# Heads before chunks: reordering ScalarE and VectorE at the end of the first block's attention, with one TensorE wait moved later

## The chip, the cores and the metric

The kernel runs on one core of a Trainium2 chip. Its time is the device time of one execution in microseconds (us); the figure compared is the median over runs. TensorE (PE) multiplies, VectorE (DVE) and ScalarE (ACT) prepare its operands and empty its banks, SyncE (SP) issues the loads of weights. Each of these engines works through its own list of instructions in order, and semaphores tie the lists together.

## The reference, cut to what matters

Two transformer blocks follow one another on a sequence of 256 tokens of width 2048. The change lies in the first block, between its input projection and its output projection:

```
h = rmsnorm(x, pre_mix_g)
q_a, k_a, v_a, q_b, k_b, v_b, f_b = split(h @ w_in)
o_a = swa_sink_attention(q_a, k_a, v_a, sinks)        # 16 heads, window of 128
o_b = forgetting_attention(q_b, k_b, v_b, log_f)      # 16 heads, causal, with a decay
mix = concat(rmsnorm(o_a), rmsnorm(o_b)) @ w_out
x = x + rmsnorm(mix, post_mix_g)
```

After it come a gated feed-forward of width 5632 with a causal convolution, and the second block. All of it is float32; the output is the final x.

## The kernel before

**Matmuls in three parts.** A float32 matmul is done as three matmuls of a rounded part and a rest. Every piece of weights (1024 columns on 128 partitions, 512 KB) is loaded into `raw`, rounded into `w_hi` by ACT (line 537) and its rest put into `w_lo` by DVE (line 1067). This is `split(u)` for piece number u; a slot of four is used again once the piece four before it was multiplied. TensorE waits for `lo_ready` of a piece, and multiplies it in 12 or 24 matmuls (lines 1862 to 1864).

**Groups of pieces.** The projections are groups of eight pieces. Group 8, the last of them, holds the second half of the values `v_b`; its products lie in banks 0 and 1 until ACT (`first_values`, line 559) and DVE (`token_out`, line 1093) scale them into `vb`. That emptying is counted by `banks_free`. After group 8 comes the first half of the output projection, `w_out_a`: eight pieces, called W0 to W7 here, of which W0 to W3 go to banks 2 and 3, W4 to W7 to banks 0 and 1. `early` is the number of W0.

**Heads.** The 32 attention heads are a pipeline that is laid between the pieces. On TensorE `head(i)` does the scores of head i (lines 2023, 2026), the turning of the probabilities of head i-2 (line 2037) and the values of head i-3 (lines 2051 to 2053). On DVE it does `bias(i)` (lines 1184 to 1194), then the reciprocal of i-1 (line 1207) and the scaling of output i-3 into `work` (line 1212). On ACT it copies the turned probabilities of i-2 out of their bank (line 645) and takes the exponentials of i (lines 657 to 660). So the values of head i-3 on TensorE wait (`out_done`) until DVE has scaled the output of head i-4, which on DVE stands behind `bias(i-1)`.

**Chunks.** The outputs of heads 0 to 15, once scaled by their norm, are turned by TensorE (`out_phase`, line 2103) into banks 2 and 3, and taken out as the chunks 0 to 7 of the output projection's left operand: `sT_hi` by ACT (line 723), `sT_lo` by DVE (line 1313), counted by `loT_done`.

**The order around the change** is written out by hand. During group 8 TensorE does head 20 behind its second piece, head 21 behind the fourth, chunks 0 to 3 behind the fifth, head 22 behind the sixth, chunks 4 to 7 behind the seventh and head 23 behind the last. ACT and DVE follow with the splits three pieces ahead: splits of W0, W1 and W2 and both sets of chunks stand before the values' scaling, and head 23 behind it. Then comes "the drain": heads 24 to 34, with W0 behind head 25, W1 behind head 27, W2 behind head 29, W3, W4, W5 and W6 behind heads 31 to 34 (`EARLY`), and on ACT and DVE the splits of W3 to W7 behind the heads that `SPLITS` names. At the drain's start TensorE waits for `loT_done` of all eight chunks and for the emptied banks of group 8, before the scores of head 24.

Of the kernel before, what the change touches and what calls it, by code (L numbers as in the profile page):

```python
# [28 lines left out]
KC = D // P  # L29
# [5 lines left out]
NH = 16  # L35
# [20 lines left out]
SLOTS = 4  # L56
# [12 lines left out]
GROUP = {}  # L69
# [7 lines left out]

EARLY = {25: 1, 27: 1, 29: 1, 31: 1, 32: 1, 33: 1, 34: 1}

SPLITS = ({24: 3, 26: 4, 28: 5, 31: 6, 33: 7}, {24: 3, 26: 4, 28: 5, 32: 6, 34: 7})  # L80

# [21 lines left out]
READER = [GROUP[n][0] for n in ("q_a", "w_out_a", "w_up", "gla_qk", "xk", "w_out2", "xq")]  # L105
# [10 lines left out]
def build(nc, A, out):  # L116
    with ExitStack() as ctx:
# [140 lines left out]
        hi_ready, lo_ready, mm_done = sem("hi_ready"), sem("lo_ready"), sem("mm_done")  # L258
        banks_free = sem("banks_free")
# [12 lines left out]
        tr_done, hiT_done, loT_done = sem("tr_done"), sem("hiT_done"), sem("loT_done")  # L272
# [64 lines left out]
        def evacuated(g, off=0):  # L337

            return EVACUATIONS[g + 1] + off
# [184 lines left out]
        def _(act):  # L524
# [143 lines left out]
            def head(i):  # L668
                if 2 <= i < 2 * NH + 2:
                    probs_copy(i - 2)  # L670
                if i < 2 * NH:
                    exps(i)
                if i == 19:
                    for b in range(NB):
                        out_squares(range(0, NH), b, stat[:, 4 + 2 * b:5 + 2 * b])
                if i == 20:
                    act.wait_ge(swa_mean, 1)
                    act.activation(half_stat(0), half_stat(0), ACT.Sqrt).then_inc(swa_root, 1)
                if i in (27, 28):
                    out_squares(range(NH, 24), i - 27, part_sq[:, i - 27, 0:1])  # L680
                if i == 2 * NH + 1:
                    for b in range(NB):
                        out_squares(range(24, 28), b, part_sq[:, b, 1:2])
                    warm(2, ACT.Sqrt)
                if i == 2 * NH + 2:
                    for b in range(NB):
                        out_squares(range(28, 2 * NH), b, part_sq[:, b, 2:3])
# [29 lines left out]
            def out_phase(chunks):  # L717

                at = GAIN_AT["grp"]
                for c in chunks:  # L720
                    if c % 2 == 0:
                        act.wait_ge(tr_done, (KC + c) // 2 + 1)
                    ins = act.activation(out_t(c)[0], bank[pair_bank(1, c // 2)][:, c % 2 * S:(c % 2 + 1) * S], ACT.Copy,
                                         scale=gains[:, at + c:at + c + 1])
                    if c % 2:
                        ins.then_inc(hiT_done, 1)

            def last_sides(j, n):
                if j % 2:
                    head(4 * n + j // 2)  # L730
                elif n == 5 and j >= 4:
                    out_phase(range(2 * j - 8, 2 * j - 4))

            for n, g in enumerate(range(3, 9)):
                group(g, side=lambda j, n=n: last_sides(j, n), take=(lambda g=g: first_values(g)) if g in GROUP["v_b"] else None)

            early = FIRST_PIECE[GROUP["w_out_a"][0]]
            for i in range(24, 2 * NH + 3):
                head(i)
                if i in SPLITS[0]:  # L740
                    split(early + SPLITS[0][i])
            act.wait_ge(mean_ready, 2)
# [90 lines left out]
            for i in range(2):  # L833
                for e in range(2):
                    g = GROUP["w_down"][e]
# [33 lines left out]
            g = GROUP["gla_v"][0]  # L869
# [38 lines left out]
            for n in range(6):  # L908
                g = GROUP["sb_q"][0] + n
# [32 lines left out]
            for n, name in enumerate(("gla_g", "sgu_u", "sgu_v", "sgu_g")):  # L942
                g = GROUP[name][0]
# [6 lines left out]
            for n in range(2):  # L950
                g = GROUP["sb_g"][n]
# [20 lines left out]
            g = GROUP["xk"][0]  # L972
            group(g)
            copy_out(xkT[:, 0:2, :].rearrange("p a b -> p (a b)"), g)
            g = GROUP["xv"][0]
# [13 lines left out]
            for e in range(4):  # L989
                g = GROUP["w_out2"][e]  # L990
# [16 lines left out]
            g = GROUP["xq"][0]  # L1007
# [33 lines left out]
            for e in range(4):  # L1041
                g = GROUP["xo"][e]
# [15 lines left out]
        def _(dve):  # L1058
# [156 lines left out]
            def head(i):  # L1215
                if i == 20:
                    dve.wait_ge(squares, 6)
                    dve.tensor_scalar(half_stat(0), half_stat(0), 1.0 / D_SWA, EPS, ALU.mult, ALU.add).then_inc(swa_mean, 1)
                if i < 2 * NH:
                    bias(i)  # L1220
                if 1 <= i <= 2 * NH:
                    recip(i - 1)
                if 3 <= i < 2 * NH + 3:
                    normalise(i - 3)
                if i == 20:
                    dve.wait_ge(swa_root, 1)
                    dve.reciprocal(half_stat(0), half_stat(0)).then_inc(swa_rstd, 1)
                    dve.wait_ge(swa_rstd, 1)
                    for c in range(2):
                        for b in range(NB):  # L1230
                            dve.tensor_scalar(work[:, b, c * W:(c + 1) * W], work[:, b, c * W:(c + 1) * W], head_factor(b, c), None,
                                              ALU.mult).then_inc(scaled, 1)
# [74 lines left out]
            def out_phase(chunks):  # L1307

                at = GAIN_AT["grp"]
                for c in chunks:  # L1310
                    if c % 2 == 0:
                        dve.wait_ge(hiT_done, (KC + c) // 2 + 1)
                    dve.scalar_tensor_tensor(out=out_t(c)[1], in0=bank[pair_bank(1, c // 2)][:, c % 2 * S:(c % 2 + 1) * S],
                                             scalar=gains[:, at + c:at + c + 1], in1=out_t(c)[0].bitcast(F32),
                                             op0=ALU.mult, op1=ALU.subtract).then_inc(loT_done, 1)

            def last_sides(j, n):
                if j % 2:
                    head(4 * n + j // 2)
                elif n == 5 and j >= 4:  # L1320
                    out_phase(range(2 * j - 8, 2 * j - 4))

            def projected(g):
                name = PLAN[g][0]
# [5 lines left out]
                else:  # L1330
                    k_halves(g, 4 * e)

            for n, g in enumerate(range(3, 9)):
                group(g, side=lambda j, n=n: last_sides(j, n), take=lambda g=g: projected(g))

            early = FIRST_PIECE[GROUP["w_out_a"][0]]
            for i in range(24, 2 * NH + 3):
                head(i)
                if i in SPLITS[1]:
                    split(early + SPLITS[1][i])  # L1340
            dve.wait_ge(out_done, 2 * NH)
# [517 lines left out]
        def _(pe):  # L1859
# [230 lines left out]
            def out_phase(quads):  # L2090

                for q in quads:
                    if q == 0:
                        pe.wait_ge(banks_free, evacuated(READER[1] - 2))
                    if q == 2:
                        pe.wait_ge(loT_done, KC + 4)
                    if q in (0, 2, 4):
                        pe.wait_ge(scaled, 2 * (q // 2) + 2)
                    if q == 6:
                        pe.wait_ge(scaled_act, 2)  # L2100
                    for c in (2 * q, 2 * q + 1):
                        for b in range(NB):
                            ins = pe.transpose(bank[pair_bank(1, q)][:, c % 2 * S + b * P:c % 2 * S + (b + 1) * P],
                                               work[:, b, c * P:(c + 1) * P], ident[:, :])
                    ins.then_inc(tr_done, 1)

            def out_piece(g, j, k0):

                u, pair = FIRST_PIECE[g] + j, 2 * (g % 2)
                pe.wait_ge(lo_ready, u + 1)  # L2110
                hi, lo = wide(w_hi, u % SLOTS, 2, W), wide(w_lo, u % SLOTS, 2, W)
                for c in range(2):
                    k = k0 + 2 * j + c
                    pe.wait_ge(loT_done, KC + max(k + 1, 4))
                    a_hi, a_lo = out_t(k)
                    for b in range(NB):
                        ins = three(bank[pair + b][:, :], a_hi[:, b * P:(b + 1) * P], a_lo[:, b * P:(b + 1) * P],
                                    hi[:, c, :], lo[:, c, :], k == 0, k == KC - 1)
                ins.then_inc(mm_done, 1)

            def last_sides(j, n):
                if j % 2:
                    head(4 * n + j // 2)
                elif n == 5 and j >= 4:
                    out_phase(range(j - 4, j - 2))

            for n, g in enumerate(range(3, 9)):
                group(g, "tok" if g in GROUP["v_b"] else "T", side=lambda j, n=n: last_sides(j, n))
            pe.wait_ge(loT_done, KC + 8)
            pe.wait_ge(banks_free, evacuated(READER[1] - 1))  # L2130
            early = 0
            for i in range(24, 2 * NH + 3):
                head(i)
                for _ in range(EARLY.get(i, 0)):
                    out_piece(GROUP["w_out_a"][early // 4], early % 4, 0)
                    early += 1
            out_phase(range(4, 8))
# [273 lines left out]
```

## Time and profile before

| | |
|---|---|
| median of 3 runs | 1655.26 us (1655.14 to 1655.6) |
| the profiled execution's own time | 1655.94 us |
| its span, first to last instruction | 1654.0 us |
| TensorE busy | 1629.1 us, 98% of the span |
| VectorE busy | 1031.5 us, 62% |
| ScalarE busy | 866.6 us, 52% |

The span is 1.94 us shorter than the execution's time; what lies around it is not in the trace. The median of the runs is 0.68 us below the profiled execution. The busy time of TensorE says little by itself, because the ends of matmuls are modelled and overlap; where it stands still, and for what, is read from its waits and from the order of its instructions in time.

### The profile page before, as it was taken

What the parts mean: (1) busy time and instruction counts of PE and PEld (TensorE: products, weight loads), DVE (VectorE), ACT (ScalarE), POOL (GpSimd) and SP (SyncE); (2) the same over time, 40 slices, a digit from 0 to 9 for tenths busy, and PEclk for the clock granted to TensorE, in tenths of its full rate; (3) what the DMA queues carried; (4) which work ended last, traced back from release to release, by engine and by line L of the source; (5) the groups of instructions that cost most, each with busy time, mean ns of one, the idle gap of its engine ahead of it and who ended that gap; (6) DMA issues with size and microseconds to landing.
All of it is one profiled execution on the core that took longest, in us unless ns stands there. A gap on an engine that the chain in (4) does not pass through costs nothing.

```text
span 1654.0 us, 28292 instructions
## 1 busy us (share of the span) xinstructions
PE 1629.1 (98%) x11082; PEld 1489.6 (90%) x11082; DVE 1031.5 (62%) x1479; ACT 866.6 (52%) x1251; POOL 19.2 (1%) x43
## 2 busy tenths in 40 slices
PE   9999999999999999999999999999999999999996
PEld 8999988889999999999998888888998888898895
DVE  5566665666777777666764444465666455776555
ACT  6454556555555555454454444354433795655455
POOL 3000000000000000000000000010000000000000
PEclk9999999999999999999999999999999999999999
DMA  8654542646666666666665665565656557655551
GB/s 263 176 157 137 156 129 90 203 142 193 196 193 190 188 185 188 192 200 203 193 216 181 198 204 184 183 183 153 188 170 178 153 155 242 188 173 176 181 184 64
DMA packets 155599, 294.88 MB, mean 178 GB/s; under 512 B 13460, under 2 KB 16200, under 8 KB 154872
## 3 DMA queue, kind: packets, MB, share of 16 engines
q1 hardware_dynamic: 154632, 289.76, 56.9%
q0 software_dynamic: 848, 3.90, 0.6%
q8 instruction: 61, 1.00, 0.2%
q14 instruction: 26, 0.21, 0.0%
q10 hardware_dynamic: 32, 0.01, 0.0%
HBM read 291.53 MB, written 2.10 MB: 178 GB/s over the span
## 4 chain that ended last, share of the span: by engine, by line
PE 94%; DVE 3%; ACT 2%; DMA 1%; issue 1%; ACTq 0%; SPq 0%; DVEq 0%
PE bank L1862 29%; PE bank L1863 29%; PE bank L1864 29%; DMA raw<-in_w_in 1%; PE upper L2020 1%; DVE w_lo L1067 1%; PE upper L2250 1%; PE upper L2037 0%; PE upper L2023 0%; ACT w_hi L537 0%; PE upper L2053 0%; PE upper L2052 0%; PE upper L2294 0%; DVE x_tok L1497 0%; PE upper L2051 0%
## 5 line engine op out<-in xcount | busy, mean ns | idle before, releaser
L1067 DVE TENSOR_TENSOR w_lo<-raw,w_hi 128x1024 fp32r<-128x1024 f32 (+2 forms) x548 | 655.4, 1209 | 487.4 <-ACT w_hi L537 483.2
L537 ACT ACTIVATE w_hi<-raw 128x1024 fp32r<-128x1024 f32 (+2 forms) x548 | 565.8, 1047 | 506.4 <-PE bank L1864 489.9
L1862 PE MATMUL bank<-hT_hi,w_hi 128*128 128x256 f32 x2176 | 605.8, 278 | 3.2 <-DVE hT_lo L1142 1.5
L1863 PE MATMUL bank<-hT_lo,w_hi 128*128 128x256 f32 x2176 | 602.1, 277 | 0.0
L1864 PE MATMUL bank<-hT_hi,w_lo 128*128 128x256 f32 x2176 | 602.0, 277 | 0.0
L1862 PEld LDWEIGHTS bank<-hT_hi,w_hi 128*128 128x128 f32 x2176 | 408.8, 188 | 5.0 <-issue 2.8
L1863 PEld LDWEIGHTS bank<-hT_lo,w_hi 128*128 128x128 f32 x2176 | 408.9, 188 | 0.0
L1864 PEld LDWEIGHTS bank<-hT_hi,w_lo 128*128 128x128 f32 x2176 | 408.9, 188 | 0.0
L1862 PE MATMUL bank<-w_hi,hT_hi 128*128 128x512 f32 (+1 forms) x640 | 249.4, 390 | 0.0
L1864 PE MATMUL bank<-w_hi,hT_lo 128*128 128x512 f32 (+1 forms) x640 | 246.2, 385 | 0.0
L1863 PE MATMUL bank<-w_lo,hT_hi 128*128 128x512 f32 (+1 forms) x640 | 245.9, 384 | 0.0
L1864 PEld LDWEIGHTS bank<-w_hi,hT_lo 128*128 128x128 f32 x640 | 120.1, 188 | 24.2
L1862 PEld LDWEIGHTS bank<-w_hi,hT_hi 128*128 128x128 f32 x640 | 120.2, 188 | 23.2 <-issue 0.3
L1863 PEld LDWEIGHTS bank<-w_lo,hT_hi 128*128 128x128 f32 x640 | 120.3, 188 | 22.8
L1864 PE MATMUL bank<-w_hi,g_lo 128*128 128x512 f32 x352 | 137.0, 389 | 0.0
L1863 PE MATMUL bank<-w_lo,g_hi 128*128 128x512 f32 x352 | 137.0, 389 | 0.0
L1862 PE MATMUL bank<-w_hi,g_hi 128*128 128x512 f32 x352 | 136.9, 389 | 0.0
L1862 PEld LDWEIGHTS bank<-w_hi,g_hi 128*128 128x128 f32 x352 | 66.1, 188 | 13.9
L1863 PEld LDWEIGHTS bank<-w_lo,g_hi 128*128 128x128 f32 x352 | 66.1, 188 | 13.8
L1864 PEld LDWEIGHTS bank<-w_hi,g_lo 128*128 128x128 f32 x352 | 66.1, 188 | 13.5
L1434 DVE SCALAR_TENSOR_TENSOR cv_val<-bank,coef,cv_val 128x255 f32<-128x255 f32 (+1 forms) x88 | 36.3, 475 | 22.1 <-ACT cv_val L804 22.1
L1434 DVE SCALAR_TENSOR_TENSOR cv_gate<-bank,coef,cv_gate 128x255 f32<-128x255 f32 (+1 forms) x88 | 36.3, 474 | 22.1 <-ACT cv_gate L804 22.1
(397 smaller groups left out, 1261.6 us busy)
## 6 DMA issues: line engine op xcount, KB each, us to landing
raw<-in_w_in SPq DMA_DIRECT2D x180, 512.0 KB, 3.9
raw<-in_w_up SPq DMA_DIRECT2D x176, 512.0 KB, 4.4
raw<-in_w_down SPq DMA_DIRECT2D x80, 512.0 KB, 4.2
raw<-in_w_out SPq DMA_DIRECT2D x64, 512.0 KB, 4.3
raw<-in_w_xkv SPq DMA_DIRECT2D x16, 512.0 KB, 4.3
raw<-in_w_down SPq DMA_DIRECT2D x16, 256.0 KB, 3.1
raw<-in_w_xq SPq DMA_DIRECT2D x8, 512.0 KB, 3.7
raw<-in_w_xo SPq DMA_DIRECT2D x8, 512.0 KB, 3.7
```

What stands on the lines that cost most here:

```text
L537: act.activation(w_hi[:, s, at:at + n], raw[:, s, 0:n], ACT.Copy).then_inc(hi_ready, 1)
L1067: dve.tensor_tensor(w_lo[:, s, at:at + n], raw[:, s, 0:n], w_hi[:, s, at:at + n].bitcast(F32), ALU.subtract).then_inc(lo_ready, 1)
L1434: ins = dve.scalar_tensor_tensor(out=cv[:, ft, back:S], in0=ps[:, 0:S - back], scalar=coef[:, e, tap, ft:ft + 1], in1=cv[:, ft, back:S], o ...
L1862: pe.matmul(o, l_hi, r_hi, start=start, stop=False, skip_group_check=True)
L1863: pe.matmul(o, l_hi, r_lo, start=False, stop=False, skip_group_check=True)
L1864: return pe.matmul(o, l_lo, r_hi, start=False, stop=stop, skip_group_check=True)
L2020: ins = pe.matmul(o[:, lo:hi], qaT[:, h // 2, b * P:(b + 1) * P], ka2[:, h // 8, h % 2, 0:n], start=True, stop=True)
L2250: ins = pe.matmul(bank[4 + 2 * b + h % 2][:, t * P:(t + 1) * P], src[po:po + HD, 1, t, b * P:(b + 1) * P], src[po:po + HD, 0, t, qb * P:(q ...
```

## The change

On ACT and DVE the last projection (group 8) is no longer done by `group`. The splits of its own pieces stay with heads 20 and 21 between them. Then come chunks 0 to 3, head 22, the split of W0, heads 23 and 24, chunks 4 to 7, the split of W1, head 25, the values' scaling (`first_values`, `projected`), the split of W2, head 26, the split of W3, head 27, the split of W4, heads 28 and 29, and the split of W5. The splits of W6 and W7 stay where they were. On TensorE no matmul moves: the wait for the chunks goes from the scores of head 24 to the first matmul of W0, behind head 25, and the wait for the banks of group 8 goes to the first matmul of W4, behind head 32.

```diff
-SPLITS = ({24: 3, 26: 4, 28: 5, 31: 6, 33: 7}, {24: 3, 26: 4, 28: 5, 32: 6, 34: 7})
+SPLITS = ({22: 0, 24: 1, 25: 2, 26: 3, 27: 4, 29: 5, 31: 6, 33: 7}, {22: 0, 24: 1, 25: 2, 26: 3, 27: 4, 29: 5, 32: 6, 34: 7})
...
-            for n, g in enumerate(range(3, 9)):
+            for n, g in enumerate(range(3, 8)):
                 group(g, side=lambda j, n=n: last_sides(j, n), take=(lambda g=g: first_values(g)) if g in GROUP["v_b"] else None)
...
             early = FIRST_PIECE[GROUP["w_out_a"][0]]
-            for i in range(24, 2 * NH + 3):
+            for j in range(5):
+                split(early - 8 + j + SLOTS - 1)
+                last_sides(j - 1, 5)
+            out_phase(range(4))
+            for i in range(22, 2 * NH + 3):
                 head(i)
+                if i == 24:
+                    out_phase(range(4, 8))
+                if i == 25:
+                    act.wait_ge(mm_done, early)
+                    first_values(GROUP["v_b"][1])
                 if i in SPLITS[0]:
                     split(early + SPLITS[0][i])
...
-            pe.wait_ge(loT_done, KC + 8)
-            pe.wait_ge(banks_free, evacuated(READER[1] - 1))
             early = 0
             for i in range(24, 2 * NH + 3):
                 head(i)
                 for _ in range(EARLY.get(i, 0)):
+                    if early == 0:
+                        pe.wait_ge(loT_done, KC + 8)
+                    if early == 4:
+                        pe.wait_ge(banks_free, evacuated(READER[1] - 1))
                     out_piece(GROUP["w_out_a"][early // 4], early % 4, 0)
                     early += 1
```

DVE has the same edit as ACT, with `projected` in place of `first_values` and `SPLITS[1]`, in which the splits of W6 and W7 stand behind heads 32 and 34. `last_sides` loses its branch for the chunks.

TensorE, the end of head 23 and the start of head 24 before (names in brackets are the semaphores an instruction waits for):

```order
L2051 MATMUL upper<-vb,probsT 128x64 [waits out_done,probsT_copied]
L2052 MATMUL upper<-vb,probsT 128x64
L2053 MATMUL upper<-vb,probsT 128x64
L2023 MATMUL upper<-kbT,qbT 128x128 [waits biased_done,banks_free,loT_done]
L2026 MATMUL upper<-cT,eye 128x128
```

and after the change, where all line numbers of TensorE are 15 higher:

```order
L2066 MATMUL upper<-vb,probsT 128x64 [waits out_done,probsT_copied]
L2067 MATMUL upper<-vb,probsT 128x64
L2068 MATMUL upper<-vb,probsT 128x64
L2038 MATMUL upper<-kbT,qbT 128x128 [waits banks_free,biased_done]
L2041 MATMUL upper<-cT,eye 128x128
```

The wait for `loT_done` has left the scores of head 24; the `banks_free` that stays there is that of an earlier group (7).

ACT from chunks 4 to 7 on, before: the values' scaling, heads 23 and 24 (each from its L645), the split of W3:

```order
L723 ACTIVATE sT_hi<-bank,gains 128x256 x4
L559 ACTIVATE vb<-bank,stat 128x512
L645 ACTIVATE probsT<-upper 128x384
L657 ACTIVATE stat<-stat 128x2
L658 ACTIVATE probs,stat<-biased,stat 128x128
L660 ACTIVATE probs,stat<-biased,stat 128x256
L645 ACTIVATE probsT<-upper 128x384
L657 ACTIVATE stat<-stat 128x2
L658 ACTIVATE probs,stat<-biased,stat 128x128
L660 ACTIVATE probs,stat<-biased,stat 128x256
L537 ACTIVATE w_hi<-raw 128x1024
```

and after, from the same chunks on: the split of W1, head 25, the values, the split of W2, head 26:

```order
L723 ACTIVATE sT_hi<-bank,gains 128x256 x4
L537 ACTIVATE w_hi<-raw 128x1024
L645 ACTIVATE probsT<-upper 128x384
L657 ACTIVATE stat<-stat 128x2
L658 ACTIVATE probs,stat<-biased,stat 128x128
L660 ACTIVATE probs,stat<-biased,stat 128x256
L559 ACTIVATE vb<-bank,stat 128x512
L537 ACTIVATE w_hi<-raw 128x1024
L645 ACTIVATE probsT<-upper 128x384
L657 ACTIVATE stat<-stat 128x2
L658 ACTIVATE probs,stat<-biased,stat 128x128
L660 ACTIVATE probs,stat<-biased,stat 128x256
```

Where two heads stood between splits, there is now a split behind heads 24, 25, 26 and 27 alike. ACT at heads 27 and 28, as a piece of the difference (L591 are the squares that both heads carry for the norm):

```order
 L660 ACTIVATE probs,stat<-biased,stat 128x256
 L591 ACTIVATE junk,part_sq<-work 128x512
+L537 ACTIVATE w_hi<-raw 128x1024
 L645 ACTIVATE probsT<-upper 128x384
 L657 ACTIVATE stat<-stat 128x2
```

The split of W4 now stands between heads 27 and 28, and its partner on DVE before `bias(28)`.

## Rows read from the trace of the kernel before

**Rows 1.** The page: span, and busy time by engine.

```profile
span 1654.0 us, 28292 instructions
...
PE 1629.1 (98%) x11082; PEld 1489.6 (90%) x11082; DVE 1031.5 (62%) x1479; ACT 866.6 (52%) x1251; POOL 19.2 (1%) x43
```

**Rows 2.** The longest thing that TensorE waited for: total, times, longest (us).

```profile
PE upper L2023 <- DVE sT_lo L1313: 2.4, 1, 2.4
```

**Rows 3.** Timeline of TensorE, head 23 to W0: start, us, instruction [idle before].

```profile
242.15 0.38 PE L2023 MATMUL upper<-kbT,qbT 128*128 128x128 f32 x2
...
243.36 0.33 PE L2051 MATMUL upper<-vb,probsT 128*128 128x64 f32 x2
...
243.75 0.39 PE L2053 MATMUL upper<-vb,probsT 128*128 128x64 f32 x2
246.51 0.58 PE L2023 MATMUL upper<-kbT,qbT 128*128 128x128 f32 x2 [2.37 <-DVE sT_lo L1313]
...
249.97 0.52 PE L2023 MATMUL upper<-kbT,qbT 128*128 128x128 f32 x2
...
251.91 0.47 PE L1862 MATMUL bank<-w_hi,sT_hi 128*128 128x512 f32 x1
```

**Rows 4.** Stretches: us, busy by engine (PE first), then granted clock (1.00 full), DMA share, GB/s.

```profile
242.00:246.50 4.50, 2.14 (x17) 1.93 (x16) 3.55 (x7) 3.33 (x7) 0.00 (x0) 1.00 0.29 94
246.50:250.00 3.50, 3.49 (x16) 3.32 (x16) 3.16 (x13) 1.57 (x6) 0.00 (x0) 0.53 0.19 71
360.00:362.00 2.00, 1.05 (x8) 0.70 (x8) 2.00 (x2) 0.00 (x0) 0.00 (x0) 1.00 0.08 31
```

**Rows 5.** Timeline of DVE, 244 to 253.3 us: chunks, values, head 24, split.

```profile
244.09 1.65 DVE L1313 SCALAR_TENSOR_TENSOR sT_lo<-bank,gains,sT_hi 128x256 fp32r<-128x256 f32 x4
245.66 0.74 DVE L1093 TENSOR_SCALAR vb<-bank,stat 128x512 f32<-128x512 f32 x1
...
248.41 0.74 DVE L1184 SCALAR_TENSOR_TENSOR biased<-upper,c,foxm 128x128 f32<-128x128 f32 x2 [0.20 <-PE upper L2026]
...
252.09 1.23 DVE L1067 TENSOR_TENSOR w_lo<-raw,w_hi 128x1024 fp32r<-128x1024 f32 x1 [1.58 <-ACT w_hi L537]
253.23 0.73 DVE L1184 SCALAR_TENSOR_TENSOR biased<-upper,c,foxm 128x128 f32<-128x128 f32 x2
```

**Rows 6.** Timeline of DVE, one undelayed head (22).

```profile
239.27 0.73 DVE L1184 SCALAR_TENSOR_TENSOR biased<-upper,c,foxm 128x128 f32<-128x128 f32 x2
...
240.69 0.17 DVE L1194 TENSOR_SCALAR stat<-stat 128x2 f32<-128x2 f32 x1
...
240.87 0.29 DVE L1212 TENSOR_TENSOR work<-upper,stat 128x128 f32<-128x128 f32 x1
```

**Rows 7.** Timeline of ACT: chunks and values; head 24 and a split; squares.

```profile
242.82 1.54 ACT L723 ACTIVATE sT_hi<-bank,gains 128x256 fp32r<-128x256 f32 x4
244.25 0.70 ACT L559 ACTIVATE vb<-bank,stat 128x512 f32<-128x512 f32 x1
244.82 0.51 ACT L645 ACTIVATE probsT<-upper 128x384 f32<-128x384 f32 x1
...
250.03 0.20 ACT L657 ACTIVATE stat<-stat 128x2 f32<-128x2 f32 x1 [0.50 <-DVE stat L1194]
...
251.02 1.04 ACT L537 ACTIVATE w_hi<-raw 128x1024 fp32r<-128x1024 f32 x1
...
263.28 0.61 ACT L591 ACTIVATE junk<-work 128x512 bf16<-128x512 f32 x1
```

**Rows 8.** Timeline of TensorE: end of W0, then the starts of W1, W2, W3.

```profile
254.76 0.38 PE L2023 MATMUL upper<-kbT,qbT 128*128 128x128 f32 x2
...
258.50 0.48 PE L1862 MATMUL bank<-w_hi,sT_hi 128*128 128x512 f32 x1
...
265.45 0.47 PE L1862 MATMUL bank<-w_hi,sT_hi 128*128 128x512 f32 x1
...
272.65 0.48 PE L1862 MATMUL bank<-w_hi,sT_hi 128*128 128x512 f32 x1
```

More of the change, by code:

```diff
@@ L728, in last_sides @@
             def last_sides(j, n):
-                if j % 2:
+                if j % 2 and j > 0:
                     head(4 * n + j // 2)
-                elif n == 5 and j >= 4:
-                    out_phase(range(2 * j - 8, 2 * j - 4))
-            for n, g in enumerate(range(3, 9)):
+            for n, g in enumerate(range(3, 8)):
                 group(g, side=lambda j, n=n: last_sides(j, n), take=(lambda g=g: first_values(g)) if g in GROUP["v_b"] else None)
             early = FIRST_PIECE[GROUP["w_out_a"][0]]
-            for i in range(24, 2 * NH + 3):
-                head(i)
+            for j in range(5):
[3 more added lines that the diff above has]
+            for i in range(22, 2 * NH + 3):
+                head(i)
+                if i == 24:
[3 more added lines that the diff above has]
+                    first_values(GROUP["v_b"][1])
                 if i in SPLITS[0]:
@@ L1317, in last_sides @@
             def last_sides(j, n):
-                if j % 2:
+                if j % 2 and j > 0:
                     head(4 * n + j // 2)
-                elif n == 5 and j >= 4:
-                    out_phase(range(2 * j - 8, 2 * j - 4))
             def projected(g):
@@ L1331, in projected @@
                     k_halves(g, 4 * e)
-            for n, g in enumerate(range(3, 9)):
+            for n, g in enumerate(range(3, 8)):
                 group(g, side=lambda j, n=n: last_sides(j, n), take=lambda g=g: projected(g))
             early = FIRST_PIECE[GROUP["w_out_a"][0]]
-            for i in range(24, 2 * NH + 3):
-                head(i)
+            for j in range(5):
+                split(early - 8 + j + SLOTS - 1)
+                last_sides(j - 1, 5)
+            out_phase(range(4))
+            for i in range(22, 2 * NH + 3):
+                head(i)
+                if i == 24:
+                    out_phase(range(4, 8))
+                if i == 25:
+                    dve.wait_ge(mm_done, early)
+                    projected(GROUP["v_b"][1])
                 if i in SPLITS[1]:
```

## The prediction

> **What bounds the kernel now.** I read the page first: TensorE is busy 98% of a span of 1654.0 us [rows 1], so a change can give or take only where it stands still or runs at a lower clock. The list of its waits puts one stop above all others: 2.4 us before line 2023, the scores of a head [rows 2]. The timeline shows the place. Head 23 starts at 242.15, its values at 243.36 and their last pair at 243.75; with 0.22 us for that pair TensorE is through at 243.97. Head 24 starts at 246.51 [rows 3], 2.54 us later. The row names the chunks, but they ended at 245.66 plus about 0.1; the values' scaling on DVE ended at 245.66 + 0.74 = 246.40 [rows 5] and was the last of the three things waited for. Then the view by stretches: the granted clock before the pause is full (2.4 GHz), behind it 0.53, that is the lower level of 1.2 GHz nearly throughout [rows 4]. Head 24 took 249.97 - 246.51 = 3.46 us where head 23 took 1.82: 1.64 us lost. So the stop costs 2.54 + 1.64 = 4.2 us, and that is all that the moved wait can return.
>
> **Part 1: the wait is moved behind head 25.** No matmul moves. Head 24 starts at 243.97: its scores need only `bias(22)`, done at 240 [rows 6]. A head on TensorE has 1.21 us to its values and 0.61 of values [rows 3]. On DVE `bias(i)` takes 1.62 us until ACT can begin the exponentials (248.41 to 250.03), and the output of head i-3 is scaled 240.87 + 0.29 - 239.27 = 1.89 us after `bias(i)` began; DVE is free again 1.8 after it [rows 5 to 7]. ACT needs 0.99 us for the exponentials (250.03 to 251.02) [rows 7]. `bias(23)` starts as its scores end, at 243.2, `bias(24)` at 245.1; the exponentials of 24 begin at 246.7 and end at 247.7. Only then come chunks 4 to 7 on ACT: four in 244.25 - 242.82 = 1.43 us, to 249.1; DVE follows with four in 1.57 us, the last pair when ACT's has landed at 249.25, done at 250.2 [rows 5, 7]. TensorE is through with head 25 at 247.7 (its values wait until 247.1 for the output of head 21, behind `bias(24)`). W0 starts at 250.3, behind a pause of 2.6 us, against 251.91 before [rows 3]. So the pause isn't removed, it is moved by two heads; what is gained to here is 1.6 us. As the pause is as long as the old one, I let the clock fall in it too: W0 then takes about 4.4 instead of 2.85 (251.91 to 254.76) [rows 3, 8] and ends at 254.7, where it ended before. That nothing is left of the gain doesn't matter, by part 2.
>
> **Part 2: a split behind each of heads 24 to 27.** ACT rounds a piece behind the exponentials of a head, DVE takes the rest, and its next `bias` is queued behind that. Around such a split the two engines work one after the other, not side by side: 1.62 + 0.99 + 1.07 (251.02 to 252.09) + 1.14 (252.09 to 253.23) = 4.82 us from one `bias` to the next [rows 5, 7]. Before, such a link came every second head, with a head of 1.8 us between: 6.6 us for two heads, and TensorE needs 2 x 1.82 + 2.85 = 6.5 for two heads and a piece. The engines were in balance: W1 starts 6.59 after W0, W2 6.95 after W1 [rows 3, 8]. Now there are three such links in a row, against 3.2 us of TensorE per head.
>
> - DVE ends the chunks at 250.2, does the split of W1 (1.14, already rounded), and begins `bias(25)` at 251.4. Exponentials 253.0 to 254.0; values' scaling on ACT 244.82 - 244.25 = 0.57 [rows 7], to 254.6; split of W2; `bias(26)` at 254.6 + 1.07 + 1.14 = 256.8. DVE's own part of the scaling (0.7) lies beside the exponentials and costs nothing.
> - The values of head 24 on TensorE wait for the output of head 23, which DVE scales behind `bias(26)`: 256.8 + 1.89 + 0.1 = 258.8. W1 starts at 259.4, against 258.50 [rows 8]: 0.9 late. With the clock down until 253.7 TensorE arrives there at 257.8 and would still wait 1.0 us, without the fall 2.35: the first fall costs nothing.
> - `bias(27)` at 256.8 + 4.82 = 261.6. Head 27 carries a square of 0.61 [rows 7] and now the split of W4: `bias(28)` at 261.6 + 4.82 + 0.61 = 267.1. The values of head 26 wait for that plus 2.0, 269.1; W2 at 269.7, against 265.45: 4.3 late.
> - Behind head 28 no split: `bias(29)` at 268.9, behind the split of W5 `bias(30)` at 268.9 + 1.62 + 0.2 + 0.99 + 1.07 + 1.14 = 273.9. The values of head 28 go at 275.9, W3 at 276.6, against 272.65 [rows 8]: 3.9 late. From here to W7 TensorE sets the pace and the order of before is kept, so what is lost stays lost: +3.9 to +4.0. The feed-forward behind it neither waits less nor works less.
>
> **The clock behind the third pause.** Before W2 TensorE would stand 1.3 us for the copied probabilities of head 26 (ACT copies them behind the split of W4, at 266.2), work 0.33, and stand 2.35 for the output of head 25: 3.6 of 4.0 us idle. No stretch of before shows a pause of that kind; the bounds are the stretch at 360 to 362 us, where 0.95 us idle left the clock at 1.00, and the pause of 2.54 us after which it fell [rows 4]. So the cost lies between 0 and what head 24 lost, 1.64, less the 0.35 that TensorE would wait anyway for the values of head 28: 1.3. I take 1.3, since the longer pause is the nearer row.
>
> The Trainium skill ("TensorE: Matmul & The Clock Gate", section "Terms") puts the penalty of a stretch at the lower level at half its length, wherever it lies. At head 24 the trace agrees: 1.64 us lost in some 3.4. Taken for the changed kernel it would charge three falls at some 1.6 each, +4.8 on the 4.0; the walk above charges only the last one, since the first two lie beside a wait for DVE.
>
> **Small parts.** The splits of W0 and W1 come later (239.4 and 249.1) and are still ready 8 us or more before their matmuls: nothing. The later wait for banks 0 and 1 asks at W4 (about 280) for what is done at 254.7: nothing. A load needs `lo_ready` of four pieces before; W5's goes out at about 251.4 and is needed at 271.7: nothing. If that cover went, it would be up to the landing time of a load.
>
> **The sum.** -1.6 (W0 earlier), taken back and turned to +4.0 at W3, +1.3 for the clock: +5.3. Against the profiled execution's own 1655.94 (span 1654.0 and 1.94 around it) that is 1661.2; that execution lies 0.68 above the median of the runs, 1655.26, so a median of 1660.6.
>
> **Rivals.**
> - *Chain without the third fall.* Same walk, clock stays full: +4.0, 1659.3. For it: the 1.3 and 2.35 us are two pauses, each shorter than the old one. Against: only 0.33 us of work between them.
> - *The chain is shorter than its links.* If the squares and splits slip into waits that I place elsewhere, and each of the three links from `bias(25)` to `bias(28)` loses 0.7 us or more, it is +2 or less: 1655.3 to 1658.5, no difference that can be told. Against: the link of 4.82 is read in one piece.
> - *Faster: the moved wait pays.* If DVE got to `bias(26)` by about 255 instead of 256.8 and to `bias(28)` by 263, TensorE would never wait for an output behind W0, and the 1.6 of part 1 would remain: 1653.7; with a clock that doesn't fall, up to 4.2: 1651.1. It decides at the values of head 24: before 257.9 the change wins, later it loses. Against it: from `bias(25)` to `bias(28)` ACT and DVE need 15.7 us one after the other, TensorE for three heads 3 x 3.2 = 9.6.
> - *Every fall costs its half.* If the falls behind the first and second pause were not hidden, 4.0 + 3 x 1.64 = +8.9: 1664.2. For it stands the rule named above. Against: TensorE waits behind both for something that DVE ends at a time of its own.
>
> **How the numbers follow.** Chances: forecast 0.45, no third fall 0.28, shorter chain 0.17, faster 0.05, every fall 0.05. About 0.2% (3.3 us) is what a measurement of this kernel can tell from no change. Slower by more: 0.45 + 0.26 + 0.05 = 0.76; within: 0.17 + 0.02 = 0.19; faster 0.05. The range leaves out the faster rival, the last one and the low half of the shorter chain: 1657.1 to 1662.3.
>
> **What would show it.** In the changed kernel's timeline: head 24 directly behind head 23; a pause of 2.6 us before W0, ended by `sT_lo`; one of 1 to 2.4 us before the values of head 24 and one of over 2 before those of head 26, both ended by `work` on DVE (line 1220); `bias` to `bias` 4.8 us apart at heads 26 and 27; W3 3.9 us or more later than before. A granted clock under 1 behind W2 decides for the forecast against the first rival. I am wrong if the values of head 24 run before 257.9, or if W3 starts before 275.

## The result and the profile after

Six runs of the changed kernel gave a median of 1661.39 us (1660.36 to 1663.18), six of the kernel before 1655.29 (1655.03 to 1656.77): ratio 1.0032, 95% interval 1.0021 to 1.0043, so 3.5 to 7.1 us slower. Forecast were 1660.6 and slower. A second comparison on another chip gave 1660.78 against 1656.33 (ratio 1.0027, 1.0017 to 1.0037). The profiled execution took 1660.36 us, its span is 4.6 us longer than [rows 1].

The page of the changed kernel, span and busy time:

```profile
span 1658.6 us, 28291 instructions
...
PE 1631.2 (98%) x11082; PEld 1490.7 (90%) x11082; DVE 1031.7 (62%) x1479; ACT 866.9 (52%) x1251; POOL 19.4 (1%) x43
```

The work is the same, to 2 us of TensorE's busy time. What TensorE waited for (total, times, longest):

```profile
PE bank L1877 <- DVE sT_lo L1321: 2.3, 1, 2.3
PE upper L2066 <- issue: 2.1, 1, 2.1
PE upper L2066 <- DVE work L1220: 2.0, 1, 2.0
```

In place of the one stop of [rows 2] there are three: at the chunks (now before W0), and twice at line 2066, the values of a head. The middle one has no releaser named; the timeline of DVE below gives it. TensorE's timeline, head 23 to W3:

```profile
241.65 0.38 PE L2038 MATMUL upper<-kbT,qbT 128*128 128x128 f32 x2
...
243.26 0.39 PE L2068 MATMUL upper<-vb,probsT 128*128 128x64 f32 x2
243.48 0.44 PE L2038 MATMUL upper<-kbT,qbT 128*128 128x128 f32 x2
...
247.13 0.39 PE L2068 MATMUL upper<-vb,probsT 128*128 128x64 f32 x2
249.80 0.50 PE L1877 MATMUL bank<-w_hi,sT_hi 128*128 128x512 f32 x1 [2.28 <-DVE sT_lo L1321]
...
258.29 0.41 PE L2066 MATMUL upper<-vb,probsT 128*128 128x64 f32 x2 [2.13 <-issue]
...
258.95 0.48 PE L1877 MATMUL bank<-w_hi,sT_hi 128*128 128x512 f32 x1
...
268.58 0.41 PE L2066 MATMUL upper<-vb,probsT 128*128 128x64 f32 x2 [1.95 <-DVE work L1220]
...
269.24 0.48 PE L1877 MATMUL bank<-w_hi,sT_hi 128*128 128x512 f32 x1
...
277.45 0.48 PE L1877 MATMUL bank<-w_hi,sT_hi 128*128 128x512 f32 x1
```

Head 24 follows head 23 at once, where [rows 3] had 2.54 us between them. Head 23 itself starts at 241.65 here and at 242.15 in [rows 3]; in the profiles of all kernels of this study it starts between 240.8 and 242.7, whatever the edit. So places are compared by their distance from the start of head 23:

| start of | before | changed | forecast | changed - before |
|---|---|---|---|---|
| W0 | 9.76 | 8.15 | 8.15 | -1.6 |
| W1 | 16.35 | 17.30 | 17.25 | +0.95 |
| W2 | 23.30 | 27.59 | 27.55 | +4.3 |
| W3 | 30.50 | 35.80 | 35.75 | +5.3 |
| W6 | 41.48 | 46.76 | | +5.3 |

Stretches of the changed kernel (us, busy by engine, then the granted clock):

```profile
242.00:249.70 7.70, 5.52 (x44) 5.16 (x42) 5.25 (x18) 5.39 (x18) 0.00 (x0) 1.00 0.23 70
249.70:256.00 6.30, 6.17 (x36) 5.22 (x36) 4.51 (x11) 3.38 (x10) 0.00 (x0) 1.00 0.25 83
256.00:259.30 3.30, 1.17 (x10) 1.00 (x9) 2.12 (x8) 1.39 (x6) 0.00 (x0) 1.00 0.46 141
259.30:262.70 3.40, 3.40 (x10) 2.65 (x9) 2.66 (x7) 1.02 (x2) 0.00 (x0) 0.51 0.12 40
269.50:273.00 3.50, 3.50 (x10) 2.72 (x10) 1.51 (x5) 2.65 (x9) 0.00 (x0) 0.51 0.08 29
```

The clock fell to 1.2 GHz behind the second and the third pause, not behind the first. Counted from the end of the work before them (the last pair of values plus 0.22 us, or the last turning plus 0.33), the three pauses last 2.45, 2.3 and 2.1 us. And DVE, from one `bias` to the next, with the split and the scaled output between:

```profile
250.90 0.74 DVE L1192 SCALAR_TENSOR_TENSOR biased<-upper,c,foxm 128x128 f32<-128x128 f32 x2
...
255.15 1.23 DVE L1075 TENSOR_TENSOR w_lo<-raw,w_hi 128x1024 fp32r<-128x1024 f32 x1 [1.71 <-ACT w_hi L537]
256.29 0.74 DVE L1192 SCALAR_TENSOR_TENSOR biased<-upper,c,foxm 128x128 f32<-128x128 f32 x2
...
257.89 0.29 DVE L1220 TENSOR_TENSOR work<-upper,stat 128x128 f32<-128x128 f32 x1
...
261.12 0.74 DVE L1192 SCALAR_TENSOR_TENSOR biased<-upper,c,foxm 128x128 f32<-128x128 f32 x2
...
266.55 0.73 DVE L1192 SCALAR_TENSOR_TENSOR biased<-upper,c,foxm 128x128 f32<-128x128 f32 x2
```

The three links take 5.39, 4.83 and 5.43 us. The output that DVE scales at 257.89 lands at 258.18, and the values of head 24 start at 258.29: that is the releaser of the middle stop. The third pause runs from the turning of head 27's probabilities (266.14) to 268.58:

```profile
266.14 0.49 PE L2052 MATMUL upper<-ident,probs 128*128 128x128 f32 x3
```

### The profile page after: what moved, and what is told of

It reads as the page before. It is cut to its first block, busy times and chain, and to the rows that moved or that the text cites. A ratio compares the mean times of both kernels' runs of the same rounds, so it can differ in the third digit from the quotient of the medians.

```text
span 1658.6 us, 28291 instructions
## 1 busy us (share of the span) xinstructions
PE 1631.2 (98%) x11082; PEld 1490.7 (90%) x11082; DVE 1031.7 (62%) x1479; ACT 866.9 (52%) x1251; POOL 19.4 (1%) x43
## 4 chain that ended last, share of the span: by engine, by line
PE 95%; DVE 2%; ACT 1%; issue 1%; DMA 0%; ACTq 0%; SPq 0%; DVEq 0%
PE bank L1877 30%; PE bank L1878 29%; PE bank L1879 29%; PE upper L2035 1%; PE upper L2267 1%; PE upper L2052 1%; PE upper L2038 0%; PE upper L2068 0%; PE upper L2067 0%; PE upper L2311 0%; PE upper L2066 0%; DVE x_tok L1512 0%; DVE x_tok L1404 0%; DMA raw<-in_w_in 0%; PE upper L2391 0%
```

## The experiments

Each was timed against the kernel before on the same chip. Two comparisons of four, and a third of three, each share the runs of before. W0 to W7 are again given from the start of head 23, read from each kernel's own timeline.

**TensorE's edit alone.** The kernel before, with its wait moved:

```diff
-            pe.wait_ge(loT_done, KC + 8)
-            pe.wait_ge(banks_free, evacuated(READER[1] - 1))
...
+                    if early == 0:
+                        pe.wait_ge(loT_done, KC + 8)
+                    if early == 4:
+                        pe.wait_ge(banks_free, evacuated(READER[1] - 1))
```

> The kernel before with TensorE's edit alone: ACT and DVE keep their old order. Theory (the chain through DVE and ACT sets the pace, the wait for the chunks was in its shadow): head 24's scores start at once, but the values of head 21 still wait for probabilities that ACT copies behind the values' scaling, and W1 waits for the same output as before. W0 about 250.8 to 251.5, W1 and all behind it 0 to 1 us earlier than before (the clock's fall spared) or up to 0.6 later: -1.0 to +0.6 us, no difference that can be told. Rival (the moved wait itself makes the loss): +3 us or more. Second rival (the moved wait pays its full price): -4 us.

Measured: 1656.10 against 1655.80 us, ratio 0.9999 (0.9990 to 1.0008). Its timeline of TensorE:

```profile
244.13 0.52 PE L2037 MATMUL upper<-ident,probs 128*128 128x128 f32 x3 [0.39 <-ACT probsT L645]
247.01 0.41 PE L2051 MATMUL upper<-vb,probsT 128*128 128x64 f32 x2 [2.37 <-DVE work L1212]
```

Head 24's scores start early, and a stop as long as the old one comes back in front of its values, at `out_done`: DVE still has chunks and values to do before it can scale an output. W0 starts at 9.92, 0.6 later than the expectation's latest (251.5 less 242.15), W3 at 31.14, 0.6 later than before. The moved wait alone makes no difference that the runs can tell.

**Splits spread again.** The changed kernel with:

```diff
-SPLITS = ({22: 0, 24: 1, 25: 2, 26: 3, 27: 4, 29: 5, 31: 6, 33: 7}, {22: 0, 24: 1, 25: 2, 26: 3, 27: 4, 29: 5, 32: 6, 34: 7})
+SPLITS = ({22: 0, 24: 1, 26: 2, 28: 3, 30: 4, 31: 5, 32: 6, 33: 7},) * 2
```

> The changed kernel with its splits spread again: W0 behind head 22, W1 behind 24, W2 behind 26, W3 behind 28, W4 behind 30, W5 to W7 behind 31 to 33, on both engines; everything else as changed. Theory (three links of a head and a split in a row are the loss): the pause before W0 stays (2.6 us), the pauses before the values of heads 24 and 26 go, W1 at 257 to 258.5, W2 at 264 to 265.5, W3 at 271 to 272.6: +0.4 us against before with a full clock, +1 us if it falls once; so 4 to 6 us faster than the changed kernel. Rival (the late scaling of the values or the late chunks are the loss): stays at +5 to +6 us.

Measured: 1657.21 against 1655.80, ratio 1.0005 (0.9996 to 1.0014). TensorE at the values of head 24 and at W1:

```profile
257.75 0.39 PE L2066 MATMUL upper<-vb,probsT 128*128 128x64 f32 x2
...
258.40 0.47 PE L1877 MATMUL bank<-w_hi,sT_hi 128*128 128x512 f32 x1
```

No wait stands in front of them. W1, W2 and W3 start at 16.33, 23.28 and 30.48, within 0.02 us of before, though the pause before W0 and the late values are as in the changed kernel. Most of the loss is gone; the order of the splits was its cause. That W1 comes out where it was before has a second part: W0 starts at 8.14, 1.6 earlier than before, and in this execution the clock was down behind it, which took the 1.6 back:

```profile
250.50:254.30 3.80, 3.80 (x11) 2.93 (x11) 3.29 (x9) 1.39 (x7) 0.00 (x0) 0.55 0.38 133
```

What is left is at the end: W4 is 0.95 late, behind a wait of 0.75 us for a scaled output of DVE, and W7 2.0, of which 1.06 is a pause of 1.62 us instead of 0.56 in front of the last chunks (below). By the ratio the kernel is 0.8 us slower than before, by the medians 1.4; the expectation was 0.4 to 1 and did not see the end coming.

**Chunks 4 to 7 early.** The changed kernel with `out_phase(range(4, 8))` behind the split of W0 on ACT and DVE:

```diff
-                if i == 24:
-                    out_phase(range(4, 8))
...
                 if i in SPLITS[0]:
                     split(early + SPLITS[0][i])
+                if i == 22:
+                    out_phase(range(4, 8))
```

> The changed kernel with chunks 4 to 7 taken out on ACT and DVE behind the split of W0, before head 23, and not behind head 24; the splits stay as changed. It takes away the pause before W0 alone. Theory (the pause before W0 is worth little, since the three links of a head and a split in a row set the pace behind it, and only begin 1.4 us earlier): W0 5.6 us after the start of head 23 instead of 8.15, W1 15.9, W2 26.2, W3 33.0 with a full clock, 34.2 with a fall, against 35.8 in the changed kernel and 30.5 before: +2.5 to +3.8 us against before. Rival (the moved pause is what was lost): with it gone, within 1 us of before.

Measured: 1659.95 against 1656.59, ratio 1.0023 (1.0014 to 1.0032). TensorE's timeline:

```profile
247.42 0.48 PE L1877 MATMUL bank<-w_hi,sT_hi 128*128 128x512 f32 x1
...
254.31 0.52 PE L2052 MATMUL upper<-ident,probs 128*128 128x128 f32 x3 [0.92 <-ACT probsT L645]
256.95 0.41 PE L2066 MATMUL upper<-vb,probsT 128*128 128x64 f32 x2 [2.13 <-issue]
```

W0 starts at 5.67 without any pause, and the time comes back in front of head 24's values; W1 15.87, W2 26.19, W3 34.40, as the theory has it with a fall of the clock. Of the 2.5 us gained at W0, 1.4 are left at W3, which is still 3.9 later than before. So taking away the pause before W0 returns 1.4 of the 5.3 us lost at W3, and the links keep the rest.

**Filler in the pauses.** The changed kernel, with matmuls of ones on TensorE that nothing needs. `stay_warm(0, n)` does n of them into bank 0; the wait added with them is for the emptying of group 8 out of that bank:

```diff
+                if i == 29:
+                    stay_warm(0, 10)
                 if 2 <= i < 2 * NH + 2:
                     turn(i - 2)
+                if i == 27:
+                    pe.wait_ge(banks_free, evacuated(8))
+                    stay_warm(0, 17)
+                if i == 29:
+                    stay_warm(0, 17)
```

> The changed kernel with matmuls of ones into a free bank in the pauses of the drain: 17 before the values of head 24, 10 before the turning of head 27, 17 before the values of head 26 (some 0.11 us each); they are work that nothing needs. Theory (the clock's fall behind the pauses costs 1.3 us, DVE and ACT the other 4.0): clock full behind W1 and W2, W3 1.3 us or more earlier than in the changed kernel, +3.9 to +4.3 us against before, and the runs lie closer together than the changed kernel's 1660.4 to 1663.2. Rival (the chain alone costs 5 to 6): no gain, +5.3 or more.

Measured: 1659.51 against 1655.80, ratio 1.0021 (1.0012 to 1.0031). TensorE's timeline, and below it its stretches:

```profile
257.04 2.02 PE L1940 MATMUL bank<-ones 128*128 128x256 bf16 x17
259.33 0.41 PE L2066 MATMUL upper<-vb,probsT 128*128 128x64 f32 x2 [0.27 <-issue]
...
265.84 1.27 PE L1940 MATMUL bank<-ones 128*128 128x256 bf16 x10
...
267.30 2.02 PE L1940 MATMUL bank<-ones 128*128 128x256 bf16 x17
269.64 0.41 PE L2066 MATMUL upper<-vb,probsT 128*128 128x64 f32 x2 [0.32 <-DVE work L1220]
```

```profile
256.00:263.00 7.00, 6.68 (x45) 5.44 (x44) 4.90 (x12) 2.94 (x9) 0.00 (x0) 1.00 0.22 75
263.00:270.00 7.00, 6.68 (x55) 5.63 (x54) 4.50 (x15) 3.79 (x13) 0.00 (x0) 1.00 0.37 122
270.00:275.00 5.00, 5.00 (x33) 4.47 (x32) 2.98 (x9) 3.68 (x12) 0.00 (x0) 1.00 0.13 45
```

The clock stays full, and the runs lie within 2.0 us (the changed kernel's within 2.8). W1 and W2 start at 17.30 and 27.60, within 0.01 us of where they start in the changed kernel: the fall behind the second pause costs nothing. W3 starts at 34.39 against 35.80: the fall behind the third costs 1.41. Against before W3 is 3.89 late, with a full clock all through: that part is DVE and ACT. The time is 3.7 us above before by the medians and 3.5 by the ratio, somewhat under the 3.9 to 4.3 expected.

Beside the changed kernel on one chip:

> The changed kernel itself, unaltered, on the same chip as the next two. Theory: +4.0 us in every run from DVE and ACT, and one or more falls of the clock in most, so +4 to +7 us against before and runs that spread over 2 us or more; runs with the lowest mean clock are the slowest. Rival (the first comparison was a chance of few runs): +3 or less.

> The changed kernel with the filler matmuls of e4_filler, beside the changed kernel on one chip. Theory: 1 to 2 us faster than the changed kernel, +3.5 to +4.3 us against before. Rival (the clock costs nothing that DVE does not hide): the same as the changed kernel within 0.5 us.

Measured: changed 1660.78 (1658.83 to 1662.01), ratio 1.0027 (1.0017 to 1.0037); with filler 1658.88, ratio 1.0017 (1.0008 to 1.0026); before 1656.33. The filler is worth 1.9 us by the medians, and the expectation for it held; its distance to before is 2.6 us by the medians and 2.8 by the ratio, less than the 3.5 expected, though the interval (1.3 to 4.3) holds it. W1 to W3 are those of the first time to 0.01 us. The changed kernel's expectation held too: 4.5 us over before, runs 3.2 us apart, and the slower ones mostly those with the lower mean clock. In its second profile both slow stretches begin a little sooner, and W1 and W2 start at 17.65 and 28.00, 0.35 and 0.41 later than the first time; W3 starts at 35.81, as the first time. So at W3 the filler is worth 1.4 us both times; where the rest of the 1.9 lies is not shown.

**Squares out of the links.** In the changed kernel the two squares of ACT go from heads 27 and 28 to 30 and 31:

```diff
-                if i in (27, 28):
-                    out_squares(range(NH, 24), i - 27, part_sq[:, i - 27, 0:1])
+                if i in (30, 31):
+                    out_squares(range(NH, 24), i - 30, part_sq[:, i - 30, 0:1])
```

> The changed kernel with the two squares of heads 16 to 23 (0.61 us each on ACT) done at heads 30 and 31, not at 27 and 28, where they lie in the links. Theory (what ACT does in a link adds to it one for one): W2 0.6 us earlier than in the changed kernel (27.0 after the start of head 23, not 27.6), W3 0.7 earlier with an equal clock; 0.7 to 2 us faster than the changed kernel, so +3.3 to +5 against before. Rival (the links are not what TensorE waits for): no change.

Measured: 1660.31 against 1656.59, ratio 1.0023 (1.0013 to 1.0033). The values of head 26 start 26.31 after head 23, in the changed kernel 26.93: the square's 0.61 us came off in full. W2 missed its number (27.34, expected 27.0), because in this execution the clock was already down when those values ran; W3 is 0.6 earlier than in the changed kernel. The median can't be told from the changed kernel's; the timeline decides.

**A new order.** One string of ACT and DVE replaces the loop (c: four chunks from that number, s: split of W, h: head, v: values):

```diff
-            for i in range(22, 2 * NH + 3):
-                head(i)
...
+DRAIN = "c0 s0 h22 c4 v h23 h24 s1 h25 h26 s2 h27 h28 h29 s3 h30 h31 s4 s5 h32 s6 h33 s7 h34"
+            for w in DRAIN.split():
```

> A new order for ACT and DVE on top of the changed kernel: chunks 0 to 3, W0, head 22, chunks 4 to 7, values, heads 23 and 24, W1, heads 25 and 26, W2, heads 27 to 29, W3, heads 30 and 31, W4, W5, head 32, W6, head 33, W7, head 34 (W for the split of a piece). Theory: no more than one split in two heads, and the chunks ready before TensorE asks: no pause over 0.6 us, no fall of the clock, W0 at 248.2, W1 254.8, W2 261.8, W3 268.5, W6 279.9, against 283.63 before: -3.6 us, 1651.7. Rival (something else than order holds the drain, such as loads that come late when W4 to W6 are split in a row): no more than -1 us.

Measured: 1652.99 against 1655.80, ratio 0.9981 (0.9972 to 0.9990): faster than before, by 1.7 to 4.6 us. Up to W6 every number held to 0.12 us, less the 242.15 at which head 23 starts before (6.14, 12.77, 19.67, 26.33, and W6 at 37.69, 3.8 earlier than before). Then 1.06 were given back:

```profile
284.05 0.66 PE L2118 MATMUL upper<-ident,work 128*128 128x128 f32 x4 [1.62 <-DVE work L1366]
```

The last chunks waited 1.62 us instead of 0.56. The next two ask what the moved wait is worth in this order, and where the 1.06 come from:

> The new order of ACT and DVE (e5_order), but TensorE's waits for the chunks and for the banks of group 8 both at their old place, before the scores of head 24. Theory (where the wait stands is worth nothing once the chunks and the values are done in time; the order of the other two engines is all): both are done within 0.3 us of the end of head 23, so the same time as e5_order to 0.3 us, -3 us against before. Rival (moving the wait gives the gain): 1.5 us or more slower than e5_order.

Measured with both waits back in front of head 24: 1652.38 against 1656.59, ratio 0.9978 (0.9969 to 0.9987). W0 at 6.17, W3 at 26.38, W7 at 44.06, against 6.14, 26.33 and 44.01: within 0.05 us. Where the chunks are done in time, the place of the wait is worth nothing.

The last swap:

```diff
+DRAIN_DVE = DRAIN.replace("s7 h34", "h34 s7")
```

> e5_order with one more swap on DVE: the split of W7 behind head 34 as before the change, not in front of it. In e5_order TensorE stands 1.62 us before the last chunks, against 0.56 before, because DVE's split of W7 waits for ACT's, which stands behind the squares of head 33, and the last head's output behind both. Theory: the pause goes back to 0.56, 1.06 us faster than e5_order, -4.1 us against before, about 1651.8. Rival (ACT's own order causes it, since the squares of head 34 come behind its split of W7): no change against e5_order.

Measured: 1652.06 against 1656.59, ratio 0.9974 (0.9964 to 0.9985). Its timeline: the only wait before W0, W0 itself, and the last chunks.

```profile
245.92 0.41 PE L2067 MATMUL upper<-vb,probsT 128*128 128x64 f32 x2 [0.38 <-DVE work L1221]
...
248.47 0.48 PE L1878 MATMUL bank<-w_hi,sT_hi 128*128 128x512 f32 x1
...
283.58 0.66 PE L2119 MATMUL upper<-ident,work 128*128 128x128 f32 x4 [0.57 <-DVE work L1367]
```

The pause is 0.57 again and W7 starts at 43.02, 3.7 us earlier than before (46.74) and 9.0 earlier than in the changed kernel (52.02). So DVE's split of W7 in front of head 34 was the cause. The spread kernel has the same order at this place and the same 1.62 us; that it is the same cause there is read from that, not tested.

> e8_order_last again on one chip with the changed kernel: -3.5 to -4.5 us against before, 9 us or more faster than the changed kernel. Rival (the first comparison flattered it): -2 us or less.

Measured again: 1651.27 (1650.94 to 1651.92) against 1656.33 of before and 1660.78 of the changed kernel: ratio 0.9970 (0.9960 to 0.9981), 9.5 us under the changed kernel. This version beats both. It is 5.1 us under before, more than the 3.5 to 4.5 expected, though the interval (3.1 to 6.6) holds those; W7 is 3.8 us earlier than before (42.96), so the order of the drain accounts for 3.8.

## Why the prediction was right, step by step

- **What bounds the kernel.** Right: only TensorE's stops and its clock changed. The old stop was priced at 4.2 us; the best order gets 3.7 of them at W7.
- **Part 1, the moved wait.** Right to 0.1 us: W0 at 8.15, behind a pause of 2.45 (247.13 + 0.22 to 249.80; 2.6 forecast), 1.6 earlier than before. With TensorE's edit alone nothing is gained, so the wait had been in the shadow of DVE's own queue. Wrong in it was that the clock would fall in this pause: it stayed full in both profiles of the changed kernel. The step had priced that fall at nothing, so the sum did not feel it. The price was right: in the kernel with the squares moved the clock did fall behind this pause, and W1 started at 17.29 as without a fall; only the wait in front of the values of head 24 was shorter, 0.76 us instead of 2.13.
- **Part 2, the links.** Right: 5.39, 4.83 and 5.43 us were read where 5.4, 4.8 and 5.4 were worked out, W1 and W2 within 0.05. The spread splits brought W1 to W3 back to their old places, and the early chunks did not: the consecutive splits are the cause. The square's place in the link (0.61) is confirmed by moving it.
- **The clock behind the third pause.** Nearly right in size, wrong in its picture. It was taken as 1.3, between 0 and 1.3; the filler puts it at 1.41. But the step saw two pauses there, 1.3 and 2.35 us with 0.33 us of work between, 3.6 of 4.0 us idle. The trace has one, of 2.1 us. The walk had W1 at a full clock; the slow stretch behind the second pause made TensorE reach head 29 later (W1 to the next head 263.37 - 258.95 = 4.42 us instead of 2.85), and that filled the first of the two. Nothing in the step says that the clock falls behind a single pause of 2.1 us, so on this term luck helped. Nor did the prediction say that executions of one kernel differ in it (below).
- **The rule of the Trainium skill.** It puts the penalty of a slow stretch at half its length ("TensorE: Matmul & The Clock Gate", section "Terms"). An estimate by it for the two stretches of 3.4 us is 3.4 us together. The filler shows 0 for the first, which ends in a wait for DVE, and 1.41 for the second. Here the rule is an upper bound, and the measurement decides.
- **Small parts.** Right for the loads and for W0's and W1's splits: the list of TensorE's waits shows none for a split or a load in the drain.
- **Sum.** +5.3 at W3, as worked out. The spans differ by 4.6, mostly because this execution reached head 23 half a microsecond sooner. The medians of the first runs differ by 6.1, their ratio gives 5.3, the second comparison 4.5.
- **Rivals.** "Chain without the third fall" is what the filler kernel shows (+3.9 at W3). The shorter chain is out by the three links, none of which was shorter than worked out by more than 0.03 us. (Its stated top, 1658.5, is +3.3 and not the +2 named beside it: it holds only with the third fall's 1.3 added.) The faster one is out too: the values of head 24 ran at 16.6 after head 23, which is 258.8 on the clock of before, and 257.9 was the limit. "Every fall costs its half" is out by the filler, which finds 0 for the fall behind the second pause.

## What to carry to other kernels

A wait that heads the list may stand in the shadow of another engine's queue: move it, and the same time returns at the next semaphore from that queue. What counts is how the engines that feed TensorE interleave two kinds of work. A step that passes through ACT and back to DVE (4.8 us here) must stand no oftener than TensorE's own pace covers, here once in two heads, and each position can be worked out from one link read in the trace. Walk the order through with a dozen durations before trying it: here the walk put W0 to W3 within 0.2 us for the changed kernel, the early chunks and the new order. Two walks were further off, W0 by 0.6 with the wait alone and W2 by 0.3 with the squares moved.

## What the runs showed of the hardware

- **The clock falls behind some pauses and not behind others of the same length.** In the changed kernel pauses of 2.3 and 2.1 us were followed by 1.2 GHz for 3.4 us, and one of 2.45 us before them by none. The same pause before W0 stands in the profiles of six executions: behind it the clock stayed full in four (the changed kernel and the filler kernel, twice each) and fell in two, the spread kernel above and the one with the squares moved:

```profile
251.60:255.00 3.40, 3.40 (x12) 2.72 (x11) 2.17 (x8) 2.09 (x7) 0.00 (x0) 0.51 0.44 154
```

  What decides it is not settled here.
- **So the same program doesn't take the same time twice.** The runs of the kernel before spread from 1653.7 to 1657.7 us on one chip, and they go by the mean granted clock: the four at 0.998 average 1654.2 us, the eleven at 0.995 average 1656.8. In the changed kernel, which has three pauses that can be followed by a fall, no run was above 0.996.
- **The drain is not the only place of it.** The last order has no pause over 0.6 us in the drain. Its second set of runs lies within 1.0 us, but its first within 2.6. The profiled execution of the first set, the slowest of it (1653.39), has a fall 1370 us behind head 23, where pauses of 0.56, 0.94 and 0.27 us stand close together:

```profile
1612.00:1615.50 3.50, 3.31 (x11) 2.78 (x12) 2.05 (x6) 2.72 (x8) 0.00 (x0) 0.60 0.00 0
```

  The profile of the second set (1650.94) has the same pauses there and no fall. W7 lies within 0.06 us in both, but from the matmuls in front of these pauses (1605.39 and 1604.36) to the end of the span it is 46.2 us against 44.7. The second profile of the changed kernel has this fall too, the first hasn't. So about 1.4 us come and go there with either order of the drain, and medians of a few runs that differ by less than that say little.
- **Work that nothing needs can save time.** 44 matmuls of ones, some 5 us of them in pauses, made the changed kernel 1.9 us faster by the medians. 1.4 of it is the clock's, read at W3.
